# Two pieces of VectorE work moved in an RWKV-7 stage: scaled keys and bonus products ahead of the key norm, the last tile's gate ahead of the first chunk

## The reference, cut to what matters

```python
r, k, v, wd, ad, gd = jnp.split(u, ...)              # u: token-shifted projections
a = jax.nn.sigmoid(a0 + ad @ a_up)
g = jax.nn.sigmoid(gd) @ g_up
kk = heads(k * k_k)
kk = kk / jnp.maximum(jnp.sqrt(jnp.sum(kk * kk, -1)), 1e-12)   # unit vector per head
k = k * (1.0 + (a - 1.0) * k_a)                                # scaled key
b_h = kk * a_h
...                                                            # recurrence over tokens, in chunks of 64
y = groupnorm(y) * gn_w + gn_b
bonus = jnp.sum(r_h * k_h * r_k, axis=-1, keepdims=True) * v_h
y = (y + bonus) * g
```

## Time and profile before

| what | value |
|---|---|
| time, median of 3 runs | 1852.48 us (1852.42 to 1853.33) |
| the profiled execution | 1854.91 us, its span 1853.2 us |
| mean granted TensorE clock | 0.974 of full speed |
| TensorE matmul busy | 1740.7 us (94%) |
| VectorE, ScalarE, GpSimd busy | 1000.4, 574.0, 829.6 us |

### The profile page before, as it was taken

One profiled execution on the slowest core, in us unless ns is written; L12 is line 12 of the kernel. 1 busy time (PEld: TensorE's weight loads), 2 busy tenths in 40 slices (PEclk: granted clock), 3 DMA queues, 4 the chain that ended last, 5 costly groups with the idle time before them and its releaser, 6 DMA issues.

```text
span 1853.2 us, 26709 instructions
## 1 busy us (share of the span) xinstructions
PE 1740.7 (94%) x10754; PEld 1272.8 (69%) x10754; DVE 1000.4 (54%) x1367; ACT 574.0 (31%) x1031; POOL 829.6 (45%) x401
## 2 busy tenths in 40 slices
PE   6999989899997788999999999999999999999998
PEld 4868668777333234678777777677777688888887
DVE  6696688553111013586878889466889912222112
ACT  4342632533322213334544545653000210000000
POOL 0442246341111103133223232236898787887884
PEclk8999899999999898999999999999999999999999
DMA  8822134444999995122122222113465232332331
GB/s 296 318 101 91 57 102 137 166 178 185 391 419 419 420 414 209 63 80 91 61 84 62 91 60 77 58 58 125 171 226 210 103 103 91 97 96 91 102 103 69
DMA packets 68374, 290.65 MB, mean 157 GB/s; under 512 B 9632, under 2 KB 9632, under 8 KB 55840
## 3 DMA queue, kind: packets, MB, share of 16 engines
q1 hardware_dynamic: 61488, 271.65, 40.8%
q10 hardware_dynamic: 2160, 8.91, 1.2%
q0 software_dynamic: 4608, 8.40, 1.2%
HBM read 282.37 MB, written 14.94 MB: 160 GB/s over the span
## 4 chain that ended last, share of the span: by engine, by line
PE 71%; DMA 9%; DVE 6%; POOL 6%; issue 5%; ACT 3%; ACTq 0%; POOLq 0%; SPq 0%; DVEq 0%
PE bank L2872 69%; DMA arena<-weights_dram 8%; POOL hi_ring L2843 2%; POOL lo_ring L2845 2%; PE bank L2876 2%; POOL lo_ring L2819 1%; ACT arena L2247 1%; DVE late L3425 1%; DVE arena L2421 1%; DVE arena L3425 0%; DMA arena<-mod_weights_dram 0%; DMA arena<-y_dram 0%; DMA xT<-x_dram 0%; DVE merged_lo L2616 0%; DVE arena L2738 0%
## 5 line engine op out<-in xcount | busy, mean ns | idle before, releaser
L2872 PE MATMUL bank<-h_lo,hi_ring 128*128 128x512 f32 x648 | 255.6, 394 | 0.0
L2872 PE MATMUL bank<-arena 64*64 64x64 f32 (+5 forms) x1704 | 198.5, 369 | 38.6 <-DMA arena<-weights_dram 33.2
L3560 POOL TENSOR_TENSOR lo_ring<-ring,hi_ring 128x1024 fp32r<-128x1024 f32 x46 | 120.0, 2610 | 245.1 <-ACT hi_ring L2813 245.1
L2872 PE MATMUL bank<-mix_h_hi,lo_ring 128*128 128x512 f32 x576 | 227.4, 395 | 0.0
L2845 POOL TENSOR_TENSOR lo_ring<-ring,hi_ring 128x1024 fp32r<-128x1024 f32 x77 | 208.7, 2711 | 6.1
L2872 PEld LDWEIGHTS bank<-arena 128*64 128x64 f32 (+2 forms) x1704 | 98.9, 147 | 125.2 <-issue 109.0
L2843 POOL TENSOR_TENSOR hi_ring<-ring,col 128x1024 fp32r<-128x1024 f32 x77 | 157.1, 2041 | 61.1 <-PE bank L2872 60.5
L2872 PE MATMUL bank<-mix_h_hi,hi_ring 128*128 128x512 f32 x416 | 166.4, 400 | 4.7 <-POOL lo_ring L2845 1.5
L2421 DVE SCALAR_TENSOR_TENSOR arena<-bank,col,arena 128x511 f32<-128x511 f32 (+14 forms) x240 | 156.6, 725 | 0.0
L2872 PEld LDWEIGHTS bank<-h_lo,hi_ring 128*128 128x128 f32 x648 | 121.7, 188 | 29.2
L2872 PE MATMUL bank<-ffn_h_hi,lo_ring 128*128 128x512 f32 x352 | 138.1, 392 | 0.0
(11 more groups left out here) (464 smaller groups left out, 3982.5 us busy)
## 6 DMA issues: line engine op xcount, KB each, us to landing
ring<-weights_dram SPq DMA_DIRECT2D x200, 512.0 KB, 3.5
arena<-weights_dram SPq DMA_DIRECT2D x61, 1024.0 KB, 24.7
arena<-mod_weights_dram SPq DMA_DIRECT2D x54, 512.0 KB, 4.5
late<-mod_weights_dram SPq DMA_DIRECT2D x42, 512.0 KB, 3.5
ring<-weights_dram SPq DMA_DIRECT2D x15, 1024.0 KB, 28.6
hT<-weights_dram SPq DMA_DIRECT2D x10, 1024.0 KB, 29.0
late<-weights_dram SPq DMA_DIRECT2D x5, 1024.0 KB, 28.7
xT<-x_dram SPq DMA_DIRECT2D x4, 1024.0 KB, 6.4
```

Source lines behind the costliest of these rows:

```text
L2872: return pe.matmul(out, lhsT, rhs, start=start, stop=stop, skip_group_check=True)
L3560: pool.tensor_tensor(ring_r[:, u % RING, :], ring[:, u % RING, :], hi_unit(u).bitcast(F32), ALU.subtract).then_inc(S("split"), 1)
```

## The change

Five edits of order and one of engine; no matrix work changes.

```diff
@@ act_decays, behind the four Sigmoids that make a
+            for n in range(RW):
+                act.activation(kk[:, n, :], x_in(4 + n), ACT.Copy, scale=column("rwkv_k_k", n)).then_inc(S("kk_raw"), 1)
             act.preload_act_table_set(LN_EXP)
@@ new function
+        def dve_scaled_keys(dve, steps):
+            for n in range(RW):
+                dve.wait_ge(*at_count("kk_raw", n + 1))
+                steps.mark(dve.tensor_tensor(x_in(4 + n), x_in(4 + n), k_scale[:, n, :], ALU.mult))
+            steps.wait()
+            for n in range(RW):
+                dve.scalar_tensor_tensor(bonus[:, n, :], x_in(n), column("rwkv_r_k", n), x_in(4 + n), ALU.mult, ALU.mult).then_inc(S("bonus_in"), 1)
@@ dve_keys
-                dve.scalar_tensor_tensor(kk[:, n, :], x_in(4 + n), column("rwkv_k_k", n), kk_sides[n], ALU.mult, ALU.mult).then_inc(S("kk_unit"), 1)
-            for n in range(RW):
-                steps.mark(dve.tensor_tensor(x_in(4 + n), x_in(4 + n), k_scale[:, n, :], ALU.mult))
+                dve.tensor_tensor(kk[:, n, :], kk[:, n, :], kk_sides[n], ALU.mult).then_inc(S("kk_unit"), 1)
...
-            for n in range(RW):
-                dve.scalar_tensor_tensor(bonus[:, n, :], x_in(n), column("rwkv_r_k", n), x_in(4 + n), ALU.mult, ALU.mult).then_inc(S("bonus_in"), 1)
@@ dve_rwkv, in the 20 steps
+                if s == 18:
+                    dve.wait_ge(*at_count("bonus_b", RW))
+                    dve.wait_ge(*at_count("gate_r", RW))
+                    steps.mark(dve.tensor_tensor(bonus[:, :, 3 * P:4 * P], bonus[:, :, 3 * P:4 * P], gate_r[:, :, 3 * P:4 * P], ALU.mult))
             mod_bias(MOD_LATE, MOD_OUT)
+            steps.wait()
+            for n in range(RW):
+                steps.mark(dve.tensor_scalar(gate_r[:, n, 3 * P:4 * P], gate_r[:, n, 3 * P:4 * P], column("rwkv_gn_w", n), None, ALU.mult))
@@ dve_rwkv, end of chunk c
-                if c == 1:
-                    dve.wait_ge(*at_count("bonus_b", RW))
-                    dve.wait_ge(*at_count("gate_r", RW))
-                    steps.mark(dve.tensor_tensor(bonus[:, :, 3 * P:4 * P], bonus[:, :, 3 * P:4 * P], gate_r[:, :, 3 * P:4 * P], ALU.mult))
-                    steps.wait()
-                    for n in range(RW):
-                        steps.mark(dve.tensor_scalar(gate_r[:, n, 3 * P:4 * P], gate_r[:, n, 3 * P:4 * P], column("rwkv_gn_w", n), None, ALU.mult))
@@ the order of the calls on VectorE
             dve_key_scales(dve, steps)
+            dve_shift(dve, 9)
+            dve_scaled_keys(dve, steps)
             modulate(38, 39)
-            dve_shift(dve, 9)
             dve_keys(dve, steps)
```

## The result

| kernel | median of its runs | lowest to highest | runs |
|---|---|---|---|
| before | 1852.38 us | 1846.73 to 1855.72 | 13 |
| changed | 1839.73 us | 1833.54 to 1848.45 | 13 |

The ratio of changed to before, taken between the means, is 0.994, with a 95% interval of 0.9922 to 0.9957: the changed kernel is faster, by 12.65 us between the medians and 11.0 us between the means (8.0 to 14.4 by the interval). The forecast was 10.3 us, 1842.2 us.

The account below looks back on a forecast made before the run. TensorE, busy 94% of the span, was taken to bound the kernel, with VectorE delaying it at the projections' end and in chunk 2. Gains 6.3 + 4.0 = 10.3 us from 1852.48 gave 1842.2 us; 80% range 1838.5 to 1848.2.

Parts of the forecast that it names:

- gain of A: End of the projections: work moved ahead of the key norm's results lets TensorE start tile 13 6.3 us earlier.
- gain of B: Chunk loop: last tile's bonus and gate work moved ahead of chunk 0 gives 2.4 + 1.6 = 4.0 us.
- The copies on ScalarE: Before ScalarE's wait for TensorE's weight tile: four copies take 2.54 us at cost 0, with 3.1 us of cover.
- The scaled keys behind a lowering: VectorE ahead of the key norm: GpSimd's first lowering holds scaled keys until 216.3, not 215.15; loss 0.5 us.
- The stall that only moves, and the one that goes: VectorE behind the key norm: 2.0 us port stall moves to the second lowering; another 2.0 us leaves the products.
- The late lowering: Rival: GpSimd's third lowering misses its turn under `dve_shift(11)`; the first part's gain shrinks to 3.0 or 0.4 us; chance 0.12.
- the three chains: Ahead of tile 13: three chains end within 1.7 us of each other, so TensorE and GpSimd set the end.
- The pause in chunk 2: Chunk loop: TensorE's 2.37 us wait for VectorE's `sa` in chunk 2 goes.
- The clock behind it: Chunk 2 after TensorE's wait: the lower clock level costs 1.60 us, which goes too, though perhaps run-variable.
- only the waits: Rival: waits go but the clock gain is absent; 8.7 us, or 7 us with another clock fall; chance 0.15.
- Given back later: Rival: a later stage, such as a transfer with its own time, takes up the gain; 1849 to 1852.5 us; chance 0.09.
- Slower by the clock: Rival: TensorE without pauses from 205 to beyond 260 is held at the lower clock; 1860 us; chance 0.04.

Follow-up runs that it names:

- e3: The changed kernel again with no edit, timed against the kernel before: median 1839.47 us, ratio 0.9954.
- e11: The changed kernel a third time with no edit, timed against the kernel before: median 1841.95 us, ratio 0.9959.
- e6: The changed kernel with `modulate(38)` put back ahead of the shift of tile 9: 1835.57 us in one run.
- e5: The changed kernel with VectorE waiting for its own first eight products before the other eight: 1844.31 us in one run.
- e4: The changed kernel without ScalarE's four copies; VectorE makes the raw unit vectors ahead of the scaled keys: 1849.24 us in one run.
- e7: The kernel before plus ScalarE's four copies and the plain multiplication for the unit vectors, nothing moved: 1844.5 us in one run.
- e8: The changed kernel with tile 12 leaving out its eight matmuls with the low part of the weights: 1841.78 us in one run.
- e9: Second run of the kernel before with only the last tile's gate work moved ahead of the first chunk: median 1846.58 us, ratio 0.9987.
- e2: First run of the kernel before with only the last tile's gate work moved ahead of the first chunk: median 1849.67 us, ratio 0.9998.
- e1: First run of the changed kernel with the chunk loop as before, so only the key norm work changed: median 1845.68 us, ratio 0.998.
- e10: Second run of the changed kernel with the chunk loop as before, so only the key norm work changed: median 1846.22 us, ratio 0.9977.

## Why the prediction was right, step by step

| step, behind KS | predicted | in after |
|---|---|---|
| unit vectors start | 222.6 - 212.55 = 10.05 | 9.96 |
| `dve_shift(10)` ends | 18.05 | 17.9 |
| `dve_shift(11)` ends | 28.4 | 28.1 |
| third lowering ends | 30.05 | 29.67 |
| tile 13 starts | 30.1 | 30.03 |
| gain of A | 6.3 us | 6.34 us |
| gain of B | 4.0 us | 2.57 us here, 4.05 in e3 |
| first expert load | 10.3 us earlier | 7.86 here, 10.23 in e3 |

I had named as a sign of being wrong that the expert loads move by much less than 10 us. In the first trace they moved 7.86: 1.5 us are missing by the clock in chunk 2 and 1.05 us between A and B. In e3 and e11 they moved 10.2 and 10.3.

*The copies on ScalarE.* 2.55 us, at no cost; 3.33 us of idle time are left ahead of the weight tile. I had counted 3.1.

*The scaled keys behind a lowering.* They were held up to its end as I had put it, and the loss against the ready norm was 0.4 us (e6) where I had 0.5. It was no term of the end, as e6 shows. Of the Trainium skill's page "SBUF — State Buffer", the section "Who interferes with whom" has the lock; the words that the prediction quotes stand in its section "Summary: rules for kernel authors".

*The stall that only moves, and the one that goes.* The second lowering got in at the pause and the third found none. The rule that I read from the rows of before held in after and in e5. As a general rule it is incomplete: in e4 (at the products), e6 and e7 a lowering also got in behind the first instruction of a new line, without a pause, and in e4 another one behind the second. Had that happened at the products in after, A would have been 4.5 us or less (e5 gives 36.37 - 31.87). This is a case that my rivals didn't have: a lowering too early for VectorE, not too late for TensorE. What decides between two back-to-back instructions stays open.

*The late lowering* (0.12) didn't come: it ended 0.36 us ahead of need. The 1.7 us that I gave for the three chains measures only to the end of the last shift (1.9 us in after); TensorE needs another 1.4 us from the third bonus sum to tile 13, and so counted the chains end within 0.5 us of each other (e8).

*The pause in chunk 2.* Gone in all traces with B. *The clock behind it.* Against the 4.21 us that the chunk takes at the upper level, the fall costs 1.60 us in before, 1.57 in its repeat and 1.62 and 1.37 in the two runs of A alone; it is missing in e7. Of the nine traces without the pause only that of after has one. So it is a term that mostly goes with the pause and that one execution can have or not. The Trainium skill has the same of a kernel's start ("TensorE: Matmul & The Clock Gate", "Part 1: The HAM clock gate"), and here the rows show it deep inside. The rival *only the waits* (0.15) had 8.7 us, and A and B gave 8.91 in the trace of after, but 10.4 in e3 and in e11: right for the one execution, wrong for the other two.

*Given back later* (0.09): no, as far as the second block. From KS to the first matmul of `mix_h_hi` with `hi_ring` weights, 29 us into that block, before took 560.05 us and its repeat 559.45; A alone 549.44 and 550.98; B alone 553.77 and 553.84; both 546.6, 546.2 and 547.25. The gain there is 13 us with both, some 3 more than at the first load: the stage between takes nothing back. No trace ties these 3 us to the change: from the first load to that matmul the 14 traces take 368.5 to 374.1 us, 369.9 in e7, where nothing was moved, and 373.3 in e5, where both were. Behind that matmul the traces differ by up to 6.4 us (last section).

*Slower by the clock* (0.04): no. The granted clock is 1.00 throughout A.

*The sum.* 10.3 us, against 12.65, 9.3 and 7.9 us between the medians of three timed comparisons, or 11.0, 8.6 and 7.5 between the means. The comparison that was forecast came out 2.35 us above the term, within its own interval. With intervals of some 6 us in width the times don't test the sum more closely than that, and how near the first one came is in part luck. The sum itself is borne out by the traces, term by term. What the timing doesn't settle is the share of each part: A alone gave 3.1 and 3.65 us between medians and B alone -0.9 and 3.3, less than their marks of 6.3 and 4.0 in the traces, and together less than both kernels' gain. Their intervals reach 6.3 and 6.5 us for A, which just holds its mark, and 3.7 and 5.0 us for B, of which the first doesn't hold the 4.0. One thing bears on B: 10 of its 24 runs have a mean granted clock of 0.976 or less, and 6 of the 53 of before on the same two chips, but also 6 of the 31 of the changed kernel, which has B too. Whether the parts gain less by themselves or the runs fell so stays open.

## What to carry to other kernels

Look for an engine's idle time ahead of a late input, and ask which of its next instructions need that input; where one of them only stands behind because it would overwrite something, a copy on an idle engine frees it. Price the move by the first instruction of the busiest engine that waits for that chain, and stop where the next chain ends: here 5.1 us less work behind the norm and 2.0 us less stall became 6.3 us, and 1.9 us less on TensorE after that gave 0.3. Where VectorE and GpSimd both read SBUF, an added or removed wait on one moves whole instructions of the other, and it pays to look whether the one that loses is the one with slack.

## What the runs showed that I had not expected

*One kernel's executions differ in stages that nobody touched.* From the last `mix_h_hi` matmul (second block) to the end, a trace takes one of about four lengths: 462.2 us in before, 463.5 in its repeat, 462.3 in after, 463.6 in e3, 466.1 in e9, 468.6 in e11 and 468.7 in e2. All five traces of 466 us or more (with e5 and e8) are among the nine of kernels that have B, and none among the five that don't; that may be chance, and no run tests it. Windows of 20 us that start 20 and 80 us behind that point, in B alone (e2):

```profile
1398.60:1418.60 20.00, 16.50 (x64) 12.46 (x63) 19.87 (x18) 0.63 (x1) 15.06 (x6) 0.91 0.54 184
1458.60:1478.60 20.00, 18.52 (x59) 11.50 (x58) 10.87 (x16) 8.41 (x12) 1.63 (x2) 0.82 0.00 1
```

and in before:

```profile
1411.00:1431.00 20.00, 16.50 (x70) 12.59 (x70) 19.87 (x17) 0.63 (x1) 16.06 (x7) 1.00 0.52 184
1471.00:1491.00 20.00, 20.00 (x82) 14.93 (x81) 12.01 (x16) 7.31 (x10) 7.79 (x5) 1.00 0.14 53
```

The granted clock is 1.00 in both windows of before and 0.91 and 0.82 in those of e2. The stretch ahead of KS differs too, from 206.5 to 213.8 us over all traces. Each of the two is about 7 us, as large as either part of the change.

*TensorE's own stall in the pair products.* Ahead of their last matmuls TensorE stands still and no semaphore ends it ("issue" in the row at 249.03). It is 1.81 to 2.43 us in the seven traces of after, e1, e3, e6, e8, e10 and e11, and 1.17 to 1.72 us in the seven of before, its repeat, e2, e4, e5, e7 and e9. In before it was 1.54 us and in after 2.14, so 0.6 us of A was taken back there. The second group all had a wait of TensorE for VectorE ahead of tile 13, and the first had none, except e8, which had one of 1.13 us and the longest stall. So such a wait alone doesn't explain it, and the cause stays open.
